# A two-layer attention trunk on one core: layer 0's scores from high and low parts, first output tiles a slot earlier, last tile stored in halves

## The reference

```
layer 0:  u = rms_norm(x) * (1 + scale) + shift;  q, k, v, z = split(u @ a_w_in)
          q, k normed per sub-head (16 sub-heads of 64), 8 heads of two sub-heads
          s = q k^T / 8 - slope * distance, causal; p = softmax(s)
          a = (p_sub0 - lambda * p_sub1) @ v;  o = rms_norm(a) * 0.8 * silu(z)
          h1 = x + gate * (o @ a_w_out)
shared:   k_s, v_s from rms_norm(h1) modulated @ w_kv  (2 K/V heads)
layer 1:  q, z from rms_norm(h1) modulated @ b_w_in; 16 heads attend to the last 128 keys,
          a sink logit joins each softmax;  out = h1 + gate * ((o * silu(z)) @ b_w_out)
```

## Time and profile before

| | |
|---|---|
| median of 3 runs | 1199.85 us (1197.83 to 1202.57) |
| profiled execution, its own time | 1202.08 us |
| its span | 1200.0 us |
| TensorE busy | 1127.0 us, 94% |
| VectorE busy | 725.6 us, 60% |
| ScalarE busy | 667.6 us, 56% |
| GpSimd busy | 157.3 us, 13% |
| chain that ended last | TensorE 84%, VectorE 6%, ScalarE 3% |

### The profile page before, as it was taken

One profiled execution on the slowest core, in us unless ns is written; L12 is line 12 of the kernel. 1 busy time (PEld: TensorE's weight loads), 2 busy tenths in 40 slices (PEclk: granted clock), 3 DMA queues, 4 the chain that ended last, 5 costly groups with the idle time before them and its releaser, 6 DMA issues.

```text
span 1200.0 us, 18984 instructions
## 1 busy us (share of the span) xinstructions
PE 1127.0 (94%) x5928; PEld 873.0 (73%) x5928; DVE 725.6 (60%) x2353; ACT 667.6 (56%) x2041; POOL 157.3 (13%) x294
## 2 busy tenths in 40 slices
PE   1488999999999999999998999999999999999997
PEld 1356777777767777776766788878878888788886
DVE  6776767767677676777766454665555555556221
ACT  4566566665656566565654544666666666665010
POOL 1110011101101011110110111211111111110212
PEclk9989999999999999999998999999999999998999
DMA  9621222222222222222221633301111111113542
GB/s 362 219 76 51 87 80 86 90 77 86 80 86 75 91 86 74 78 70 94 86 80 53 209 114 115 123 19 40 40 41 40 41 40 45 49 41 108 156 140 88
DMA packets 65460, 108.44 MB, mean 90 GB/s; under 512 B 5584, under 2 KB 34384, under 8 KB 65104
## 3 DMA queue, kind: packets, MB, share of 16 engines
q1 hardware_dynamic: 65360, 107.23, 28.5%
HBM read 90.43 MB, written 16.78 MB: 89 GB/s over the span
## 4 chain that ended last, share of the span: by engine, by line
PE 84%; DVE 6%; ACT 3%; issue 3%; DMA 2%; SPq 1%; POOL 0%; POOLq 0%; DVEq 0%; ACTq 0%
PE ps_p L546 15%; PE ps_p L548 13%; PE ps_p L547 13%; PE ps_s L601 6%; PE ps_o L652 5%; PE ps_p L592 4%; PE ps_p L590 4%; PE ps_p L591 4%; PE ps_o L730 4%; PE ps_t L670 3%; PE ps_o L774 2%; PE ps_s L710 2%; PE ps_t L757 2%; DMA ada_in<-ada_w 1%; PE ps_o L627 1%
## 5 line engine op out<-in xcount | busy, mean ns | idle before, releaser
L546 PE MATMUL ps_p<-w_hi,u_hi 128*128 128x512 f32 x768 | 336.7, 438 | 21.9 <-DVE u_lo L1198 21.9
L548 PE MATMUL ps_p<-w_hi,u_lo 128*128 128x512 f32 x768 | 303.9, 396 | 0.0
L547 PE MATMUL ps_p<-w_lo,u_hi 128*128 128x512 f32 x768 | 302.8, 394 | 0.0
L546 PEld LDWEIGHTS ps_p<-w_hi,u_hi 128*128 128x128 f32 x768 | 146.0, 190 | 85.9 <-ACT gbuf L870 28.6
L548 PEld LDWEIGHTS ps_p<-w_hi,u_lo 128*128 128x128 f32 x768 | 145.4, 189 | 32.8
L547 PEld LDWEIGHTS ps_p<-w_lo,u_hi 128*128 128x128 f32 x768 | 146.8, 191 | 17.5
L932 ACT ACTIVATE e<-e,negm 128x256 f32<-128x256 f32 (+7 forms) x128 | 98.3, 769 | 97.6 <-DVE negm L1263 96.5
L1152 DVE TENSOR_TENSOR w_lo<-raw,w_hi 128x512 fp32r<-128x512 f32 x120 | 82.9, 699 | 87.6 <-ACT w_hi L843 87.6
L479 POOL TENSOR_SCALAR gbuf<-gbuf 128x128 f32<-128x128 f32 (+1 forms) x96 | 36.3, 378 | 555.0 <-ACT gbuf L870 555.0
L601 PE MATMUL ps_s<-kT,qT 64*128 64x512 f32 (+3 forms) x384 | 89.7, 544 | 7.2 <-DVE negm L1263 4.6
L652 PEld LDWEIGHTS ps_o<-va,pT 128*128 128x128 f32 x576 | 72.4, 193 | 17.1 <-issue 13.8
(11 more groups left out here) (179 smaller groups left out, 2007.7 us busy)
## 6 DMA issues: line engine op xcount, KB each, us to landing
adabuf<-ada_w SPq DMA_DIRECT2D x48, 512.0 KB, 3.9
raw<-w_a SPq DMA_DIRECT2D x76, 256.0 KB, 4.0
raw<-w_b SPq DMA_DIRECT2D x44, 256.0 KB, 3.1
ada_in<-ada_w SPq DMA_DIRECT2D x7, 1024.0 KB, 13.3
x_in<-x SPq DMA_DIRECT2D x8, 512.0 KB, 12.4
oa_scratch<-gbuf SPq DMA_DIRECT2D x64, 64.0 KB, 1.6
late<-oa_scratch SPq DMA_DIRECT2D x8, 512.0 KB, 4.3
stage<-x SPq DMA_DIRECT2D x8, 512.0 KB, 4.8
```

Of the source, the lines that this page charges most:

```text
L546: pe.matmul(o, u_hi[:, c, t], w_hi[par][:, c, :], start=(c == 0), stop=False)
L547: pe.matmul(o, u_hi[:, c, t], w_lo[par][:, c, :], start=False, stop=False)
L548: mm = pe.matmul(o, u_lo[:, c, t], w_hi[par][:, c, :], start=False, stop=(c == KD - 1))
```

## The change

**Scores.** ScalarE's two copies now write high parts in `float32r`, `kT_hi` (where `kT` is) and `qT_split[:, :, 0, :]`. VectorE subtracts them from the same PSUM values and writes the low parts, `kT_lo` (in halves of `gbuf`'s rows that layer 0 leaves unused) and `qT_split[:, :, 1, :]`; this is added behind the combine of every slot and counts up `a_low`, for which the scores now wait. A chunk of scores is three rounds, each of one product per sub-head: high keys x high queries, high keys x low queries, low keys x high queries.

**First output tiles.** In both layers `out_rows(n0, 0)` and `transposed` for tile 0 go from drain slot 2 to drain slot 1 (on ScalarE and VectorE ahead of the weight splits). The first half of tile 0's product goes from slot 3 to slot 2: chunks 0 to 3 ahead of the second chunk of scores (in layer 1 ahead of the value products), chunks 4 to 7 ahead of the last transposes of e.

**Last tile.** For the last tile of layer 1 VectorE adds the residual per half (`last_sum`), and SyncE stores each half when it is ready. A few semaphores are merged.

```diff
+        kT_hi = over(kT_at, "kT_hi", [P, SEQ], F32R)
+        qT_split = over(qT_at, "qT_split", [P, 2, 2, P], F32R)
...
+        kT_lo = over(gbuf_at, "kT_lo", [P, NT, 2, P], F32R)[:, :, 1, :]
...
-                    if n >= 0:
+                    if n == NT - 1 and not with_next:
+
+                        for h in range(2):
+                            t = slice(h * FW, (h + 1) * FW)
+                            sp.wait_ge(c_end, h + 1)
+                            sp.dma_start(dst[n * P:(n + 1) * P, t],
+                                         adabuf[:, (n % 2) * D + h * FW:(n % 2) * D + (h + 1) * FW]).then_inc(c_st[n % 2], 16)
+                    elif n >= 0:
...
-                for n in range(NT):
+                for n in range(NT - 1 if n0 else NT):
                     yo = adabuf[:, (n % 2) * D:(n % 2 + 1) * D]
...
-            def out_half(n0, unit, n, h):
+            def out_half(n0, unit, n, h, chunks=range(KD)):
...
-                    for sub in range(2):
-                        d = slice(sub * HD, (sub + 1) * HD)
-                        mm = pe.matmul(ps_s[:, sub * 512:sub * 512 + hi_k - lo_k], qT[d, it % 2, 0:P], kT[d, 0, lo_k:hi_k],
-                                       start=True, stop=True)
+                    for k in range(3):
+
+                        for sub in range(2):
+                            d = slice(sub * HD, (sub + 1) * HD)
+                            keys = kT_lo[d, lo_k // P:hi_k // P, :] if k == 2 else groups(kT_hi[d, lo_k:hi_k], P)
+                            mm = pe.matmul(groups(ps_s[:, sub * 512:sub * 512 + hi_k - lo_k], P), qT_split[d, it % 2, k % 2, :],
+                                           keys, start=(k == 0), stop=(k == 2))
                     mm.then_inc(S.s, 1)
...
                     if live(3):
-                        pe.wait_ge(S.qkT, n3 + 1)
+                        pe.wait_ge(a_low, n3 + 1)
...
+                    if not live(0) and i == 2:
+                        out_half(n0, unit_out, 0, 0, range(0, 4))
                     if live(3) and len(score_chunks(i3)) > 1:
                         scores(u3, i3, n3, 1)
                     if not live(0) and i == 3:
                         pe.wait_ge(S.m, 2 * units * UNIT_CHUNKS)
                         gate_rows(gate)
-                        out_half(n0, unit_out, 0, 0)
...
-                    if not live(0) and i == 2:
+                    if not live(0) and i == 1:
 
                         pe.wait_ge(S.ez, units * NT)
                         pe.wait_ge(S.qn, units * NT)
                         out_rows(n0, 0)
+                    if not live(0) and i == 2:
+                        out_half(n0, unit_out, 0, 0, range(4, KD))
...
-                        act.activation(kT[:, 0, i2 * P:(i2 + 1) * P], qk[:, P:2 * P], ACT.Copy)
-                        act.activation(qT[:, i2 % 2, 0:P], qk[:, 0:P], ACT.Identity, scale=gqk[:, 0:1]).then_inc(S.qkT, 1)
+                        act.activation(kT_hi[:, i2 * P:(i2 + 1) * P], qk[:, P:2 * P], ACT.Copy)
+                        act.activation(qT_split[:, i2 % 2, 0, :], qk[:, 0:P], ACT.Identity, scale=gqk[:, 0:1]).then_inc(S.qkT, 1)
+                    if not live(0) and i == 1:
+                        transposed(n0, 0)
                     split_for(S, u, i, par, live, units, U_A)
-                    if not live(0) and i in (2, 4):
-                        transposed(n0, i // 2 - 1)
+                    if not live(0) and i == 4:
+                        transposed(n0, 1)
...
+                    if live(2):
+
+                        dve.wait_ge(S.qkT, n2 + 1)
+                        qk = ps_o[:, (i2 + 1) % 2, 256:512]
+                        dve.tensor_tensor(kT_lo[:, i2, :], qk[:, P:2 * P], kT_hi[:, i2 * P:(i2 + 1) * P].bitcast(F32), ALU.subtract)
+                        dve.scalar_tensor_tensor(out=qT_split[:, i2 % 2, 1, :], in0=qk[:, 0:P], scalar=gqk[:, 0:1],
+                                                 in1=qT_split[:, i2 % 2, 0, :].bitcast(F32), op0=ALU.mult,
+                                                 op1=ALU.subtract).then_inc(a_low, 1)
+                    if not live(0) and i == 1:
+                        transposed(y_done, 0)
                     split_for(u, i, par, live, units, U_A)
...
+                def last_sum(h):
+                    n = NT - 1
+                    yo = adabuf[:, (n % 2) * D + h * FW:(n % 2) * D + (h + 1) * FW]
+                    dve.wait_ge(c_y, 2 * (n0 + n) + h + 1)
+                    dve.wait_ge(c_res, 16 * (n0 + n + 1))
+                    dve.tensor_tensor(yo, yo, stage[:, h, :], ALU.add).then_inc(c_end, 1)
```

More of the change, by code:

```diff
@@ L259, in build @@
         c_sum = sem("c_sum")
+        c_end = sem("c_end")
         c_st = [sem(f"c_st{k}") for k in range(2)]
@@ L299, in build @@
         a_osq = sem("a_osq")
+        a_low = sem("a_low")
         b_snk = sem("b_snk")
@@ L579, in out_rows @@
                         mm.then_inc(c_tr, 1)
-            def out_half(n0, unit, n, h):
+            def out_half(n0, unit, n, h, chunks=range(KD)):
                 m = n0 + n
                 at_least(pe, c_y, 2 * (m - 1) + h + 1)
-                for c in range(KD):
+                for c in chunks:
                     if h == 0 and c % 4 == 0:
@@ L592, in out_half @@
                     mm = pe.matmul(ps_p[:, h, :], lo, w_hi[h][:, c, :], start=False, stop=(c == KD - 1))
-                mm.then_inc(c_mm, 1)
+                if chunks[-1] == KD - 1:
+                    mm.then_inc(c_mm, 1)
             def attn_a(S, units, gate, n0, unit_out):
@@ L1336, in slot @@
                                                      in1=e0[:, i3 % 2, c0:c1], op0=ALU.mult, op1=ALU.add).then_inc(a_comb, 1)
+                    if live(2):
[5 more added lines that the diff above has]
+                                                 op1=ALU.subtract).then_inc(a_low, 1)
+                    if not live(0) and i == 1:
+                        transposed(y_done, 0)
                     split_for(u, i, par, live, units, U_A)
-                    if not live(0) and i in (2, 4):
-                        transposed(y_done, i // 2 - 1)
+                    if not live(0) and i == 4:
+                        transposed(y_done, 1)
                     if first and i >= 2:
@@ L1506, in output @@
                     product(n1, 0)
+                    if n1 == NT - 1 and not with_next:
+                        last_sum(0)
                     if 2 <= s < NT:
@@ L1510, in output @@
                         product(n1, 1)
+                        if n1 == NT - 1:
+                            last_sum(1)
                     elif n1 == NT - 1:
```

31 lines of the change are left out of this document (15 added, 16 removed).

## The result

The changed kernel took 1183.65 us (median of 4 runs, 1183.04 to 1185.05), the kernel before on the same chip 1201.21 us (1197.83 to 1204.72): a ratio of 0.9855, 95% interval 0.9823 to 0.9887. The profiled execution took 1183.36 us (before 1202.08), its span is 1181.6 us (before 1200.0). By the medians the gain is 17.6 us, where 16.5 was forecast from the first three times of the kernel before (median 1199.85).

The account below looks back on a forecast made before the run. TensorE was taken to bound the kernel (94% busy, 84% of the chain). Scores 7.4, passages 4.8 and 2.3, last tile 2.0 summed to 16.5 us off the 1199.85 median: 1183.4, said as 1184, range 1177 to 1192.

Parts of the forecast that it names:

- The chunks: Layer 0 score chunks on TensorE: three products shorten a head by 1.26 us, 8 heads by 10.1 us.
- The 0.23 us round: Score chunks: each round of a pair takes 0.23 us per 512 columns, as in the projection.
- the load-bound 0.106 us at 128 columns: Score chunks: a 128-column round goes by its weight load, 0.106 us, taken from layer 1's value products.
- the 0.21 us at the edges: Score chunks: going into the 64-row form and out of it costs 0.21 us per chunk.
- Rival 2: Score chunks: loads between rounds stand open, 0.21 us more on ten chunks per head, 1198 us; chance 0.04.
- rival 1: Score chunks: pairs not side by side, six rounds in a row, 42 us more, 1233 us; chance 0.05.
- VectorE gives back 0.3 us per head: Tiles of 1024 and 896 keys: low parts make VectorE late by 0.06 and 0.21 us; 2.4 us in all.
- rival 3: Tiles of 640 to 1024 keys: VectorE's lateness adds up, scores bring 0 to 3 us, say 1190; chance 0.18.
- Head 0: Tiles up to 512 keys stand on a ScalarE and VectorE chain; their 0.3 us of savings are lost.
- The passages: Into layer 1: 4.8 us saved (6.2 with clock up, 3.3 if it falls); out of it: 2.3 us.
- The bet that the dense products bring the clock back early: Passage out of layer 1: 12 dense products ahead of the values bring the clock back halfway, saving 2.3 us.
- The last tile: Layer 1's end: VectorE adds halves (about 0.7 us each), store bytes halve; 2.0 us saved (1.7 to 2.4).

Follow-up runs that it names:

- the kernel with two rounds: Changed kernel without the third pair of score products (high queries times low keys); timed once, 1175.01 us.
- the second profile after: The changed kernel run once more, unaltered; ratio 0.9847 to the kernel before, median 1184.41 us.
- their own run: Kernel before with only the scores changed (three products, low parts on VectorE); ratio 0.9929, median 1192.01 us.
- the passages kernel: Kernel before with only the first output tile moved up a slot at both passages; ratio 0.9956, median 1193.11 us.
- the one with the added transposes: Changed kernel with 640 keys scored as 384 and 256, plus 46 unused identity transposes in head 0; ratio 0.9822, median 1178.82 us.

## Why the prediction was right

1184 us was forecast and 1183.65 measured, but two of its steps were off and cancelled each other: that it came so near is in part luck.

**The chunks: right.** 0.90, 0.73, 0.56 and 0.47 us were forecast, 0.894, 0.724, 0.550 and 0.482 measured; 1.26 us per head against 1.28. The 0.23 us round, the load-bound 0.106 us at 128 columns and the 0.21 us at the edges stand up in the kernel with two rounds (0.230, 0.113). Rival 2 is out by that, rival 1 by the chunk's 0.89 us.

**VectorE gives back 0.3 us per head: wrong, it was nothing.** The low parts went into waits as forecast, but mostly not into those for the squares (2.1 us less): the 38.5 us of waits for the weights' high parts were what went. The step took 0.68 us for the two low parts, the sum of two durations of 0.34. From start to start they cost 0.46. With that, the 0.06 us late at 1024 keys become 0.16 early, and the 0.21 at 896 keys 0.01: the tile table shows both tiles shortened by what their chunks save (0.30 and 0.32 us, against 0.29 and 0.33). That rival 3 was near is shown from both sides: 0.58 us more per tile made exactly these tiles 0.58 and 0.46 us longer, and one round less brought half of its worth.

**Head 0: too small a loss.** The forecast left 0.66 us of the chunks' 1.26 there. The two profiles with one low stretch of 3.4 us each put head 1's first scores at 148.04 and 148.31 before, and at 148.09 in the second profile after: 0.1 us is left. In the first, two more low stretches cost some 2 us. So the scores brought 7.0 us by the first pair of traces and 7.8 by their own run, beside 7.4 forecast: by those traces 2.0 more in the seven steady heads (8.7 against 7 x 0.96) and 2.4 less in head 0.

**The passages: right in sum, and the mechanism is half clock.** 4.8 and 2.3 us, 7.1, were forecast, and the kernel with only this change gained 6.7. The first pair of traces shows 4.5 and 4.9, since in the second passage it set the worst case before (10.2 us low) beside the best after (none). At the same clock they are 4.1 and 0.6. For the first passage with the clock kept up the step counted 6.2 us less than the kernel before; by the passages kernel it was 5.6 (51.07 to 45.50). For the second it said that nothing there waited much, and overlooked the 2.36 us idle ahead of the transposes. The bet that the dense products bring the clock back early held in kind: with the move none of nine profiles shows more than 3.4 us low in either passage; without it they range from none (once in each passage) to 10.2. What the move gives back in clock is an average over executions.

**The last tile: right**, 2.3 us in a range of 1.7 to 2.4; the store left 1.48 us behind the last matmul, 1.5 forecast. Its cost of 0.7 us for the half was L1543's 0.69.

Left open: why five of the nine profiles with the new scores (the one with the added transposes among them) have three low stretches in head 0 and none of the five without. The low parts don't do it by themselves; that it was chance isn't excluded. Nor was the 0.2 us tried that layer 0's output gave back.

## What to carry to other kernels

Price an added instruction on a busy engine by the distance of starts in a row of its kind, not by its duration. Where two engines run a relay, the first gain goes to the bound one in full only up to the other's slack; measure that slack (double the added work, or take away more) before paying for the next gain. Where an engine's granted clock falls in one execution and not in the next, compare more than one profile on each side before a single stretch is credited to a change, and try filling an idle stretch with useless work.

## What the runs showed of the hardware

- Two 64-row halves of the array run their own streams: six products in pair order, six in sub-head order and four of the six took 0.894, 0.900 and 0.889 us.
- A round of 128 columns costs more than its columns: 0.482 us for three rounds, where the slope from 256 to 512 keys (0.172 us per 128) would give 0.38. One round more costs 0.113 us at 128 columns and 0.117 at 256, and 16 records of 64 columns start 0.106 us apart, so that at 128 columns and fewer the weight load sets the pace, as far as the rows tell.
- In head 0 and in the passages the granted clock was low for 0 to 10.2 us behind idle times of 1.5 to 2.8 us, and the same kernel differed from execution to execution by up to 6.8 us. In the one profile with 46 useless transposes in three such idle times of head 0 the clock stayed up and head 1 started 3.6 us earlier.
